# Moving the last block's input projection and recurrent chain out of the first stage and between the attention steps of block 0

## What is computed

```python
proj = h @ w_in
(xa, ya, fq, fk, fv, ff, gq, gk, gv, glow, gg) = split(proj)
xa = causal_depthwise_conv(xa, conv_w, conv_b)
out_a = rg_lru(xa, ...) * gelu(ya)                      # recurrence over time
out_b = forgetting_attention(fq, fk, fv, ff, ...)        # 6 heads of 64
out_c = gated_linear_attention(gq, gk, gv, glow, gg, ...) # 4 heads of 64, chunks of 64
x = x + gate1 * (concatenate([out_a, out_b, out_c]) @ w_out)
h = rms_norm(x, norm2_gain) * (1.0 + scale2) + shift2
gt, up = split(h @ ffn_w_gate_up)
x = x + gate2 * ((silu(gt) * up) @ ffn_w_down)
```

## Time and profile before

| | before |
|---|---|
| median of the runs | 3057.32 us |
| the profiled execution, its time | 3061.05 us |
| its span | 3059.3 us |
| TensorE (matmul) busy | 2808.7 us, 92% |
| VectorE busy | 1472.7 us, 48% |
| ScalarE busy | 1189.1 us, 39% |
| GpSimd busy | 1036.5 us, 34% |
| mean granted TensorE clock | 0.952 |

### The profile page before, as it was taken

The page is one execution under the profiler, slowest core; times in us unless marked ns, Lnnn a source line. Parts: engine busy times, 40 slices in busy tenths (PEclk is TensorE's granted clock), DMA queues, the critical chain, the costliest instruction groups (busy, mean ns, idle before and its releaser), DMA issues.

```text
span 3059.3 us, 32974 instructions
## 1 busy us (share of the span) xinstructions
PE 2808.7 (92%) x12416; PEld 2227.3 (73%) x12416; DVE 1472.7 (48%) x1881; ACT 1189.1 (39%) x1657; POOL 1036.5 (34%) x488
## 2 busy tenths in 40 slices
PE   8998999944677999999999999998999999999999
PEld 4787878822554778788677777886777877878887
DVE  3978776343455434444644355444535554431111
ACT  3333342322233535453543444534525445332222
POOL 3545454400022332234333222243332222444443
PEclk9999999975578999999999999999999999999999
DMA  7555534451445243444543445356244553433233
GB/s 261 181 173 179 170 130 134 138 178 52 121 145 156 77 125 116 135 128 145 177 140 102 133 144 152 109 183 194 87 126 132 149 148 109 152 108 96 97 97 97
DMA packets 159086, 418.65 MB, mean 137 GB/s; under 512 B 18236, under 2 KB 19788, under 8 KB 155856
## 3 DMA queue, kind: packets, MB, share of 16 engines
q1 hardware_dynamic: 156160, 411.30, 43.3%
q10 hardware_dynamic: 2768, 5.24, 0.5%
HBM read 355.56 MB, written 60.92 MB: 136 GB/s over the span
## 4 chain that ended last, share of the span: by engine, by line
PE 61%; DVE 6%; ACT 4%; issue 3%; DMA 3%; SPq 2%; POOL 1%; ACTq 0%; POOLq 0%; DVEq 0%
PE ff_acc_ps L77 15%; PE ff_acc_ps L79 15%; PE ff_acc_ps L78 15%; PE fa_st_ps L1539 2%; PE fa_o_ps L1555 2%; PE fa_s_ps L1513 2%; PE fa_st_ps L1540 1%; PE fa_o_ps L1557 1%; PE fa_s_ps L1514 1%; PE fa_o_ps L1556 1%; DMA ff_w_raw<-in_w_gate_up 1%; DVE ff_silu L1231 1%; PE fa_o_ps L1629 1%; SPq L897 1%; DVE fa_inv_sum L1268 1%
## 5 line engine op out<-in xcount | busy, mean ns | idle before, releaser
L1016 POOL TENSOR_TENSOR ff_w_lo<-ff_w_raw,ff_w_hi 128x1024 fp32r<-128x1024 f32 (+1 forms) x304 | 717.8, 2362 | 1409.0 <-PE ff_acc_ps L79 1352.5
L77 PE MATMUL ff_acc_ps<-ff_h_hi,ff_w_hi 128*128 128x512 f32 x1664 | 666.2, 400 | 48.5 <-DVE ff_h_lo L1221 14.9
L79 PE MATMUL ff_acc_ps<-ff_h_hi,ff_w_lo 128*128 128x512 f32 x1664 | 657.4, 395 | 0.0
L78 PE MATMUL ff_acc_ps<-ff_h_lo,ff_w_hi 128*128 128x512 f32 x1664 | 656.4, 394 | 0.0
L1026 ACT ACTIVATE ff_w_hi<-ff_w_raw 128x1024 fp32r<-128x1024 f32 (+1 forms) x304 | 315.3, 1037 | 827.5 <-PE ff_acc_ps L79 678.3
L77 PEld LDWEIGHTS ff_acc_ps<-ff_h_hi,ff_w_hi 128*128 128x128 f32 x1664 | 317.6, 191 | 138.6 <-issue 52.4
L79 PEld LDWEIGHTS ff_acc_ps<-ff_h_hi,ff_w_lo 128*128 128x128 f32 x1664 | 317.1, 191 | 68.7
L78 PEld LDWEIGHTS ff_acc_ps<-ff_h_lo,ff_w_hi 128*128 128x128 f32 x1664 | 317.9, 191 | 64.4 <-issue 0.7
L209 POOL TENSOR_TENSOR w_lo<-w_raw,w_hi 128x1024 fp32r<-128x1024 f32 x96 | 238.3, 2483 | 274.4 <-PE g_ps L79 208.0
L77 PE MATMUL g_ps<-h_hi,w_hi 128*128 128x512 f32 x768 | 307.0, 400 | 19.4 <-POOL w_lo L209 15.1
L79 PE MATMUL g_ps<-h_hi,w_lo 128*128 128x512 f32 x768 | 300.6, 391 | 0.0
(11 more groups left out here) (229 smaller groups left out, 3960.7 us busy)
## 6 DMA issues: line engine op xcount, KB each, us to landing
ff_w_raw<-in_w_gate_up SPq DMA_DIRECT2D x176, 512.0 KB, 3.9
w_raw<-in_w_in SPq DMA_DIRECT2D x96, 512.0 KB, 4.1
ff_w_raw<-in_w_down SPq DMA_DIRECT2D x64, 512.0 KB, 3.7
mod_w<-in_w_mod SPq DMA_DIRECT2D x24, 1024.0 KB, 5.4
fa_v<-v_split_dram SPq DMA_DIRECT2D x60, 384.0 KB
proj_dram<-stage SPq DMA_DIRECT2D x72, 256.0 KB, 3.2
ff_w_raw<-in_w_out SPq DMA_DIRECT2D x32, 512.0 KB, 4.1
fa_ks_a<-ka_dram SPq DMA_DIRECT2D x60, 256.0 KB
```

What stands on the lines that cost most here:

```text
L77: nc.tensor.matmul(out, hi, act_hi, start=first, stop=False)
L78: nc.tensor.matmul(out, hi, act_lo, start=False, stop=False)
L79: return nc.tensor.matmul(out, lo, act_hi, start=False, stop=last)
L1016: nc.gpsimd.tensor_tensor(w_lo[:, j % LO, wide], w_raw[:, j % RAW, wide], w_hi[:, j % HI, wide].bitcast(F32), ALU.subtract).then_inc(lo_re ...
```

## The change

Stage 1 runs three blocks. The 24 projection units of block 3 become slots 0 to 23 of stage 2 (kind "p"), with their copies, gates, recurrence and stores; the input of block 3 (`h_odd`), the split weights, the carry and the last three columns for the convolution are kept in memory that both stages share (`held`). Stage 1 still loads and splits the weights of the first two of these units (`GIVEN`). The prelude's slots are gone: the X steps of block 0 stand in slots 1 to 4, two to a slot, new "L" steps (the gate matmuls and sigmoids of block 3's recurrence) in slots 5 and 6, the G steps in slots 6 to 13, two to a slot, and the 32 turns of the heads in slots 15 to 22, four to a slot. Stores of X and G steps move from the start of the next slot to the end of their own. The reads of block 3's projections wait for their stores (`projected`).

```diff
-    N = NBLK * N_PROJ
+    BLOCKS = NBLK - 1
+    N = BLOCKS * N_PROJ
+    GIVEN = 2
...
+        h_odd_hi, h_odd_lo, w_hi, w_lo, carry, halo_out, rate, neg_rate = held
+        h_even_hi, h_even_lo = sb("h_even_hi", [P, KD, BLK], F32R), sb("h_even_lo", [P, KD, BLK], F32R)
+        h_hi, h_lo = (h_even_hi, h_odd_hi), (h_even_lo, h_odd_lo)
...
-                        if j + RAW < N:
+                        if j + RAW < N + GIVEN:
...
+                low(N + GIVEN - 1)
...
+    LAST, PAD, LRU_UNITS = NBLK - 1, CONV_WIDTH - 1, 2 * LRU_T
+    PSTAGES = 4
+
+    CONV_AT, MULT_AT, RATE_AT, INV_AT, ROOT_AT, GELU_AT, SCAN_AT = (2, 3, 4), (6, 7, 8), 9, (10, 11, 12), 13, 14, (15, 16, 17)
+    units = [("p", LAST, i, 0) for i in range(N_PROJ)] + [("o", 0, m, 0) for m in range(KD)]
...
+    GIVEN = 2
+    split = lambda j: j + 1 - GIVEN
+    stage_of = lambda i: (i - LRU_UNITS) % PSTAGES
...
+    X0_AT, G0_AT = 1, 1 + (X_STEPS + 1) // 2 + 1
+    A0_AT = G0_AT + GLA_T * G_STEPS // 2 + 1
     side = {}
-    begins, x_load, g_load, a_load = [], [], [], []
-    PRE = X_LEAD + X_STEPS + G_LEAD + GLA_T * G_STEPS + A_LEAD + len(turns_of(0)) + 1
-    for b in range(NBLK):
+    for s in range(X_STEPS):
+        side.setdefault(X0_AT + s // 2, []).append([("X", (0, s))])
+    side[G0_AT - 1] = [[("L", 0)], [("L", 1)]]
+    side[G0_AT] = [[("L", 2)]]
+    for s in range(GLA_T * G_STEPS):
+        side.setdefault(G0_AT + s // 2, []).append([("G", (0, s // G_STEPS, s % G_STEPS))])
+    for x, turn in enumerate(turns_of(0)):
+        side.setdefault(A0_AT + x * (N_PROJ - 1 - A0_AT) // len(turns_of(0)), []).append(turn)
+    x_load, g_load, a_load, fill_at = [0], [G0_AT], [A0_AT - 1], [A0_AT]
+    for b in range(1, NBLK):
         turns = turns_of(b)
-        lo = -PRE if b == 0 else 1 if b == 1 else at["o", b - 1, KD - 1, 0] + 1
+        lo = at["o", 0, 0, 0] + 1 if b == 1 else at["o", b - 1, KD - 1, 0] + 1
...
-            put(slot_of["X", (b, s)] + 1, ("XO", (b, s)))
+            refill(("X", (b, s)), ("XO", (b, s)))
+        if b == 0:
+            refill(("X", (0, X_STEPS - 1)), ("G", 0))
+        else:
+            put(g_load[b], ("G", b))
         for j in range(GLA_T):
-            put(slot_of["G", (b, j, G_STEPS - 1)] + 1, ("GO", (b, j)))
-    order = {"XO": 0, "GO": 0, "X": 1, "G": 1, "Q": 1, "KS": 2, "KT": 3, "O": 4}
+            refill(("G", (b, j, G_STEPS - 1)), ("GO", (b, j)))
...
+            if kind == "p":
+                return p_read, j + 1
...
+                        if b == LAST:
+                            projected(sp)
...
+                    if j == at["o", 0, 0, 0] - 1:
                         load_mix(0)
+                    if j >= 2 and units[j - 2][0] == "p" and units[j - 2][2] >= LRU_UNITS:
+                        q = units[j - 2][2]
+                        sp.wait_ge(p_read, q + 1)
+                        sp.dma_start(proj[q, :, cols(LAST)], p_stage(q)).then_inc(p_stored[stage_of(q)], 16)
+                    if kind == "p" and i - 2 in SCAN_AT:
+                        t = SCAN_AT.index(i - 2)
+                        sp.wait_ge(out_ready, t + 1)
+                        sp.dma_start(mix[t, :, cols(LAST)], r_gate[:, t]).then_inc(lru_stored, 16)
+                    if kind == "p" and i == N_PROJ - 2:
+                        sp.wait_ge(lru_stored, 16 * LRU_T)
+                        for w in range(2):
+                            residual(0, w)
...
+                    if j in MULT_AT:
+                        t = MULT_AT.index(j)
+                        pool.wait_ge(sig_done, 2 * t + 2)
+                        pool.wait_ge(conv_ready, t + 1)
+                        nc.gpsimd.tensor_tensor(u_in[:, t], u_in[:, t], conv[:, t], ALU.mult).then_inc(u_ready, 1)
...
+                def open_gates(t):
+                    act.wait_ge(gates_done, t + 1)
+                    nc.scalar.activation(r_gate[:, t], s_ps[:, bank_of(("gate0", t))], ACT.Sigmoid, bias=wcol("b_r", t)).then_inc(sig_done, 1)
+                    nc.scalar.activation(u_in[:, t], s_ps[:, bank_of(("gate1", t))], ACT.Sigmoid, bias=wcol("b_i", t)).then_inc(sig_done, 1)
+
+                def recur(i):
+                    if i == RATE_AT:
+                        act.wait_ge(sig_done, 2 * LRU_T)
+                        for t in range(LRU_T):
+                            nc.scalar.activation(inv[:, t], r_gate[:, t], ACT.Tanh, scale=rate[:, t:t + 1]).then_inc(tanh_done, 1)
+                            nc.scalar.activation(lru_decay[:, t], r_gate[:, t], ACT.Exp, scale=neg_rate[:, t:t + 1]).then_inc(lru_decayed, 1)
+                    if i == ROOT_AT:
+                        for t in range(LRU_T):
+                            act.wait_ge(arg_ready, t + 1)
+                            nc.scalar.activation(inv[:, t], inv[:, t], ACT.Sqrt).then_inc(root_done, 1)
+                    if i == GELU_AT:
+                        act.wait_ge(p_read, LRU_UNITS)
+                        for t in range(LRU_T):
+                            nc.scalar.activation(ya[:, t], ya[:, t], ACT.Gelu_apprx_tanh).then_inc(gelu_done, 1)
...
+                def evict(i):
+                    if i < LRU_UNITS:
+                        out = xa[:, i, PAD:] if i < LRU_T else ya[:, i - LRU_T]
+                    else:
+                        q = i - LRU_UNITS
+                        if q >= PSTAGES:
+                            dve.wait_ge(p_stored[q % PSTAGES], 16 * (q // PSTAGES))
+                        out = p_stage(i)
+                    dve.wait_ge(unit_done, i + 1)
+                    nc.vector.tensor_copy(out, acc_ps[:, i % GB]).then_inc(p_read, 1)
...
-                for j in range(-PRE, 0):
-                    attend(j)
-                for k in range(KD):
-                    mix_low(0, k)
                 for j in range(N + 1):
+                    if j == 1:
+                        dve.wait_ge(xc_in, 80)
                     if j >= 1:
                         kind, b, i, p = units[j - 1]
                         n = KF * b + i
                         acc = acc_ps[:, (j - 1) % GB]
+                        if kind == "p":
+                            evict(i)
+                            if i in CONV_AT:
+                                convolve(CONV_AT.index(i))
+                            if i in INV_AT:
+                                one_less_decay(INV_AT.index(i))
+                            if i in SCAN_AT:
+                                recur(SCAN_AT.index(i))
+                            if i == N_PROJ - 1:
+                                for k in range(KD):
+                                    mix_low(0, k)
...
+                def gate(t):
+                    pe.wait_ge(conv_ready, t + 1)
+                    pe.wait_ge(gates_in, 16 * LRU_T)
+                    for g in range(2):
+                        use = ("gate%d" % g, t)
+                        bank_free(use)
+                        last = nc.tensor.matmul(s_ps[:, bank_of(use)], gates[:, g, t], conv[:, t], start=True, stop=True)
+                    last.then_inc(gates_done, 1)
...
+                    if j >= GIVEN:
+                        pe.wait_ge(lo_ready, split(j))
```

More of the change, by code:

```diff
@@ L99, in project_in_and_recur @@
     MEAN0_AT, INVERT_AT = 4, 5
-    later = [(b, i) for b in range(NBLK) for i in CHUNK_AT][:MOD_CHUNKS - FIRST_CHUNKS]
+    later = [(b, i) for b in range(BLOCKS) for i in CHUNK_AT][:MOD_CHUNKS - FIRST_CHUNKS]
     chunk_at = {u: FIRST_CHUNKS + n for n, u in enumerate(later)}
@@ L225, in _ @@
                     low(j)
-                for b in range(NBLK):
+                for b in range(BLOCKS):
                     for i in range(N_PROJ):
                         j = N_PROJ * b + i
-                        if 1 <= j and j + 1 < N:
+                        if j >= 1:
                             low(j + 1)
@@ L708, in mix_and_feed_forward @@
         two = lambda n: many(n, 2)
-        h_hi, h_lo = sb("ff_h_hi", [P, KD, BLK], F32R), sb("ff_h_lo", [P, KD, BLK], F32R)
+        h_hi, h_lo, w_hi, w_lo, carry_in, halo_in, rate, neg_rate = held
+        region = ExitStack()
+        lru_there = lambda n, s: region.enter_context(nc.sbuf_tensor(n, s, F32))
+        with region:
+            xa, ya = lru_there("lru3_xa", [P, LRU_T, PAD + BLK]), lru_there("lru3_ya", [P, LRU_T, BLK])
+            conv, r_gate, u_in, inv, lru_decay, lru_state = (lru_there("lru3_" + n, [P, LRU_T, BLK]) for n in ("conv", "r_gate", "u_in", "inv", "decay", "state"))
+            gates = lru_there("lru3_gates", [P, 2, LRU_T, P])
         region = ExitStack()
@@ L945, in _ @@
-                        for w in range(2):
-                            residual(0, w)
                     for x in sorted(loads.get(j, []), key=lambda x: order[x[0]]):
                         side_load(x)
-                    if j >= 0 and j + RAW < N:
+                    if j >= GIVEN and j + RAW < N:
                         weights(j + RAW)
-                    if j >= 0:
-                        rest(j)
```

(3 more changed lines are left out.)

176 lines of the change are left out of this document (106 added, 70 removed).

## The result

The changed kernel takes 3019.26 us (median of 4, 3015.84 to 3023.98) against 3055.61 (3050.88 to 3062.19): 0.988 of the time before, 95% interval 0.9863 to 0.9898. It is faster by 36 us where 92 were forecast; the range held it by less than 1 us. The profiled execution has a span of 3022.2. Three single executions, one of the kernel before (6792.86 us), one of b1_align512 (4417.08) and one of d2_align128 (8700.66), ran in a far slower state and are left out of every number here, and since the trace of b1_align512 is of such an execution, no spacing is read from it.

What follows compares the result with a forecast made beforehand. Two stretches lie end to end, block 3 bound by TensorE and the prelude by latency; overlaid, 78.0 + 96.1 + 103.5 plus 7.3 gives 284.9 against 379.2 us, 94.3 less: median 2965 us, range 2925 to 3020.

Steps and rivals of the forecast that it cites:

- is the same: Stage 1 up to block 2's last unit (494.9 us): unchanged but for one more low part of 2.40 us.
- 2185 us, within 5: From the first "o" unit to the end: left as before, 2185 us; a changed tail would refute the forecast.
- I count some 4 us in all for this.: GpSimd's low parts slowing VectorE's steps in the moved stretch: some 4 us in all, otherwise hidden.
- The price of 58 us: Port lock between GpSimd and VectorE, a full low part paid in each of 24 units: 24 x 2.4 us, time 3020.
- Part 1: Start of stage 2 to the linear attention's first matmul: 60.4 us before, 78.0 forecast.
- Part 2: Linear attention's first matmul to the first score: 87.1 us before, 96.1 forecast, ends 75 and 120.
- One more block by GpSimd: +1: Term for the stretch from the linear attention's first matmul to the first score: 1 us more.
- The 11 us wait before the first score: TensorE stands still some 11 us during store, fill and load after the last G result, unit 14 being done.
- Part 3: The heads, first score to first "o" unit: 88.5 us before, 103.5 forecast, ends 92 and 140.
- I take 11.5: A slot of one head and one unit: TensorE 11.0 us, VectorE 10.0 us, taken as 11.5 us.
- rival (b): Longer waits from the fixed order, part at the lower clock: 2997 us, or 3020 with every low part paid; chance 0.25.
- I price all units at full clock: TensorE's matmuls in the merged stretch counted at full clock, 200 us together; windows expected above 0.85.

Runs made afterwards that it cites:

- b1_align512: Changed kernel with an unused 352-byte tile behind the shared tiles, so h_even and ff_a begin a multiple of 512 bytes from the weights: 3001.4 us.
- d2_align128: Changed kernel with an unused 224-byte tile behind the shared tiles, so h_even and ff_a begin 384 bytes past a multiple of 512 from the weights: 3015.5 us.
- c3_w8: Changed kernel with operands in step, heads' turns later and recurrence behind side steps (2982.7 us); now unit 8's raw weights issue before the linear attention's loads: 2969.5 us.

## Why the prediction was wrong, point by point

Three steps failed: the same order was taken for the same time (19 us), GpSimd's low parts were priced at 4 us (28), and the units were priced at full clock in a stretch full of waits (46 us of longer matmuls; a part of the 28 us is among them, so the three do not add up). The sum also slips in its last step: 2966.8 less 3.7 is 2963, not 2965.

**Stage 1 "is the same", the tail "2185 us, within 5".** Wrong by 5.5 and 13.5 us. The step that failed is that, the rows of all engines being the same, "I leave those 2185 us as they are". The diff moves the operands in SBUF, which the order of instructions doesn't show. The text named a changed tail and heads of over 15 us as what would refute it, and both came.

**GpSimd: "I count some 4 us in all for this."** It was 28. The 2.12 us beside 0.41 were read, and then 48 us busy of 48 in the earlier trace rows taken as proof that this hides. In that window TensorE waited for VectorE nowhere; in the moved stretch it does nine times, six of them in M. The trace of the kernel before had the same wait elsewhere, behind the first "o" unit (TensorE's waits, 874.5 to 3059 us: total, times, longest):
```profile
PE fa_s_ps L1523 <- DVE fa_m_cols L1255: 12.5, 11, 2.2
```
L1523 is M of the later blocks, and three of the casts there took 1.6 to 1.7 us beside GpSimd. The Trainium skill's page "SBUF — State Buffer" ("SBUF: two separate sides") says that a GpSimd instruction and a VectorE instruction with two SBUF inputs, or in a mode that takes both ports, share a port pair, and that the one who comes second is blocked until the other's instruction ends. The trace agrees: the multiplication and the cast end 0.55 and 0.03 us behind GpSimd's. The price of 58 us that the prediction worked out by that rule, every low part paid in full, is twice the measured one; that its 3020 stands beside the measured 3019 is chance, since 17 to 24 us of the 3019 come from the operands' place.

**Part 1, 78.0 us.** Right: 80.9, and the wait goes back to the high part of a late raw weight and the sigmoids, as written:
```profile
586.95 1.06 ACT L1091 ACTIVATE w_hi<-ff_w_raw 128x1024 fp32r<-128x1024 f32 x1 [11.35 <-DMA ff_w_raw<-in_w_in]
```
It was avoidable (c3_w8), which I did not see.

**Part 2, 96.1 us.** 105.9, and 96.9 without the other causes. "One more block by GpSimd: +1" should have been some 10. The 11 us wait before the first score came as 9.96.

**Part 3, "I take 11.5" a slot.** 15.4 to 18.5 us a slot; the bound of 16 in rival (b) was the likelier value. The term that was missing is that M stands first in its slot, behind a copy that waits for the unit's end. The 11 us of TensorE's work and the 10 us of VectorE's were set side by side as if they could lie beside each other, and at the head of a slot they can't. With M one place on and without GpSimd the last slots are 11.6 us.

**The clock: "I price all units at full clock".** For this the prediction had the windows of the earlier trace rows, at 0.94 and 1.00, where TensorE waited 3.1 us and not at all. In the moved stretch it waits 70 of 316 us, the clock is 0.82, and the 200 us of matmuls take 246. In the kernels with shorter waits (43 to 58 us) the clock is 0.86 to 0.90 and the matmuls take 231 to 239 us. So the lower clock goes with the waits, as rival (b) has it; no run changed the one without the other, and how much of each wait's price is the clock's has not been measured by itself.

Of the rivals (b) comes nearest: longer waits, part of the stretch at the lower clock, 2997 to 3020. Waits in the heads are longer, but in the sum of the three parts they are not (70.0 us for 77.6); the 38 us there are TensorE's work at the lower clock. The other 19 of the 57 us belong to no rival.
